# Split-float projections of a decoder step: three products per tile, or high-part products first

## The reference

```
h = rms_norm(x, g_pre_mix);  z = h @ w_in
o = concat(rms_norm(attention_A(z)), rms_norm(attention_B(z)))
x = x + rms_norm(o @ w_out, g_post_mix)
h = rms_norm(x, g_pre_ffn)
u = h @ w_gate;  up = h @ w_up
c = conv_b + sum(conv_w[j] * u_pad[:, j:j + L] for j in range(3))
x = x + rms_norm((gelu(c) * up) @ w_down, g_post_ffn)
```

## Time and profile before

| | |
|---|---|
| median of three runs | 1191.3 us |
| time of the profiled execution | 1191.31 us |
| its span, first to last instruction | 1189.3 us |
| mean granted TensorE clock | 0.993 |
| TensorE matmul (PE) busy | 1165.3 us, 98%, 9947 matmuls |
| TensorE weight load (PEld) busy | 1133.0 us, 95%, 9947 loads |
| VectorE (DVE) busy | 700.7 us, 59% |
| ScalarE (ACT) busy | 552.8 us, 46% |
| GpSimd (POOL) busy | 105.6 us, 9% |
| HBM read | 216.45 MB, 186 GB/s over the span |

### The profile page before, as it was taken

How to read it: one execution, slowest core, us unless ns; L and a number is a source line. 1 busy time by engine, 2 the same in 40 slices (tenths; PEclk the granted TensorE clock), 3 DMA queues, 4 the chain that set the end, 5 groups by cost and what they waited for, 6 DMA issues and landing times.

```text
span 1189.3 us, 25575 instructions
## 1 busy us (share of the span) xinstructions
PE 1165.3 (98%) x9947; PEld 1133.0 (95%) x9947; DVE 700.7 (59%) x1052; ACT 552.8 (46%) x857; POOL 105.6 (9%) x163
## 2 busy tenths in 40 slices
PE   9999999999999799999999999999999999999995
PEld 8999888988999799999999999999999999999995
DVE  6977565575475966565656565655655444454445
ACT  7545455565455654453444444444444333343331
POOL 0100110110002010010011001100110000020001
PEclk9999999999999899999999999999999999999998
DMA  9646687676555355655555555556555655555551
GB/s 332 191 154 228 236 252 232 210 235 219 169 184 181 106 157 177 205 161 192 161 191 173 180 173 181 179 173 190 176 179 173 212 177 179 181 184 180 176 159 73
DMA packets 59473, 222.21 MB, mean 187 GB/s; under 512 B 7064, under 2 KB 7264, under 8 KB 57312
## 3 DMA queue, kind: packets, MB, share of 16 engines
q1 hardware_dynamic: 55008, 196.53, 51.4%
q0 software_dynamic: 4272, 24.94, 6.3%
q10 hardware_dynamic: 144, 0.05, 0.0%
HBM read 216.45 MB, written 5.00 MB: 186 GB/s over the span
## 4 chain that ended last, share of the span: by engine, by line
PE 95%; DVE 2%; DMA 1%; ACT 1%; issue 0%; SPq 0%; POOL 0%; DVEq 0%; ACTq 0%
PE ps L1136 30%; PE ps L1137 29%; PE ps L1138 29%; PE ps L1309 1%; DMA Vk<-in_vb 1%; PE ps L1227 1%; PE ps L1290 1%; PE ps L1218 1%; PE ps L1216 1%; DMA raw<-in_w_in 1%; DVE wl L679 1%; PE ps L1245 0%; PE ps L1163 0%; DVE yT L983 0%; DVE ps L982 0%
## 5 line engine op out<-in xcount | busy, mean ns | idle before, releaser
L1136 PE MATMUL ps<-hh,wh 128*128 128x264 f32 x2080 | 599.3, 288 | 7.6 <-DVE hl L892 5.8
L1138 PE MATMUL ps<-hh,wl 128*128 128x264 f32 x2080 | 592.4, 285 | 0.0
L1137 PE MATMUL ps<-hl,wh 128*128 128x264 f32 x1952 | 557.0, 285 | 0.0
L679 DVE TENSOR_TENSOR wl<-raw,wh 128x1024 fp32r<-128x1024 f32 x363 | 438.6, 1226 | 186.7 <-ACT wh L423 186.2
L423 ACT CAST wh<-raw 128x1024 fp32r<-128x1024 f32 x363 | 374.8, 1046 | 275.7 <-PE ps L1138 271.6
L1136 PEld LDWEIGHTS ps<-hh,wh 128*128 128x128 f32 x2080 | 393.3, 189 | 19.7 <-issue 17.3
L1138 PEld LDWEIGHTS ps<-hh,wl 128*128 128x128 f32 x2080 | 392.2, 189 | 0.0
L1137 PEld LDWEIGHTS ps<-hl,wh 128*128 128x128 f32 x1952 | 368.1, 189 | 0.1
L1137 PE MATMUL ps<-gl,wh 128*128 (+1 forms) x704 | 200.4, 285 | 0.0
L1136 PE MATMUL ps<-gh,wh 128*128 (+1 forms) x704 | 200.1, 284 | 0.0
L1138 PE MATMUL ps<-gh,wl 128*128 (+1 forms) x704 | 199.6, 283 | 0.0
(11 more groups left out here) (230 smaller groups left out, 830.5 us busy)
## 6 DMA issues: line engine op xcount, KB each, us to landing
raw<-in_w_gate SPq DMA_DIRECT2D x88, 512.0 KB, 3.7
raw<-in_w_up SPq DMA_DIRECT2D x88, 512.0 KB, 4.5
raw<-in_w_down SPq DMA_DIRECT2D x88, 512.0 KB, 3.6
raw<-in_w_in SPq DMA_DIRECT2D x67, 512.0 KB, 4.9
raw<-in_w_out SPq DMA_DIRECT2D x32, 512.0 KB, 3.9
Kt<-in_kb POOLq DMA_DIRECT2D x8, 1284.0 KB, 6.3
Vk<-in_vb POOLq DMA_DIRECT2D x8, 1024.0 KB, 7.1
out_y<-yT SPq DMA_DIRECT2D x8, 264.0 KB, 2.1
```

What stands on the lines that cost most here:

```text
L679: V.tensor_tensor(wl[:, slot], raw[:, slot], wh[:, slot].bitcast(F32), ALU.subtract).then_inc(lo_ready, 1)
L1136: nc.tensor.matmul(out, a, x, start=start, stop=False)
L1137: nc.tensor.matmul(out, a, xl, start=False, stop=False)
L1138: return nc.tensor.matmul(out, b, x, start=False, stop=stop)
```

## The change

The three matmuls of a tile are split into `mm_high` (`wh` by high, then `wl` by high) and `mm_low` (`wh` by low). In `gemm` each k tile does both output tiles' `mm_high` and then both `mm_low`. In `down` a chunk does all eight `mm_high` and then all eight `mm_low`; the waits per m stay before `mm_high`, and the signals of the last chunk of the first half move with `mm_low`. `mm3` is left for the last two chunks of `w_down`, which aren't changed.

```diff
+            def mm_high(out, w, x, start):
+
+                slot, c = w
+                nc.tensor.matmul(out, wh[:, slot, c:c + P], x, start=start, stop=False)
+                nc.tensor.matmul(out, wl[:, slot, c:c + P], x, start=False, stop=False)
+
+            def mm_low(out, w, xl, stop):
+
+                slot, c = w
+                return nc.tensor.matmul(out, wh[:, slot, c:c + P], xl, start=False, stop=stop)
+
...
                     for m in range(2):
-                        ins = mm3(ps[:, bank + m, 0:TOK], (slot, 256 * k + P * m), xh[:, kt0 + k], xl[:, kt0 + k],
-                                  first and k == 0, last and k == 3)
+                        mm_high(ps[:, bank + m, 0:TOK], (slot, 256 * k + P * m), xh[:, kt0 + k], first and k == 0)
+                    for m in range(2):
+                        ins = mm_low(ps[:, bank + m, 0:TOK], (slot, 256 * k + P * m), xl[:, kt0 + k], last and k == 3)
...
                     if first and half == 1:
                         pe.wait_ge(down_v, m + 1)
-                    ins = mm3(ps[:, (m + 4) % 8, 0:TOK], (slot, P * m), gh[:, kt], gl[:, kt], first, last)
+                    mm_high(ps[:, (m + 4) % 8, 0:TOK], (slot, P * m), gh[:, kt], first)
+                for m in range(8):
+                    ins = mm_low(ps[:, (m + 4) % 8, 0:TOK], (slot, P * m), gl[:, kt], last)
                     if last and m < 7:
                         ins.then_inc(down_done, 1)
```

## The result

The changed kernel takes 1194.3 us (median of 20 runs, 1192.42 to 1195.86), against 1191.83 us for the kernel before (median of 20, 1190.36 to 1195.69). The ratio is 1.0016, with a 95% interval of 1.0009 to 1.0023; the two medians are 2.5 us apart, which is 0.21%. So it is slower by some 0.2%, at the edge of the 2.4 us that I had called no change, and clear of zero. The profiled execution took 1193.36 us with a span of 1191.6 us, 2.3 us over the span of before.

The account below looks back on a forecast made before the run. The prediction took TensorE's stream of matmuls to bound the kernel. From 1191.3 us, plus 1.4 at the border between w_down's halves and 0 for the pace, it forecast 1192.7 us, range 1185.0 to 1200.0.

Parts of the forecast that it names:

- TensorE is the bound: Whole kernel: TensorE's matmul row is busy 98% of the span, so any wait there lengthens the time in full.
- Gemm chunks: The 68 + 32 + 176 chunks of gemm: same matmuls, waits and end signals in place, so 0 us apart from the pace.
- From gate and up to down: First down chunk: the wait for up_taken comes sooner, but VectorE's read-out is still early by 0.55 us, so 0 us.
- The border: Between w_down's halves: banks finish later and are wanted sooner, so TensorE waits +1.4 us, bounds 0 and 2.0.
- The clock: TensorE's granted clock: the new idle comes in pieces too short to lower it, so 0 us.
- The pace of all chunks: Mean matmul interval in 364 chunks, less the last two: taken as unchanged, 0 us, with ends -7.3 and +7.3 us.
- case 2: All chunks: the new order settles in the slower matmul pattern, up to 1200.0 us; chance 0.33.
- Rival 3: All chunks: fewer switches between high and low settle matmuls in the quicker pattern, down to 1185.4 us; chance 0.27.
- What would show it: Signs: gate and up repeats each two chunks at 122.4 ns within 0.3; PE wait of 1 to 2 us entering the second half.
- the likeliest case: Whole kernel: the pace keeps its mean and the halves' border costs 1.4 us, 1192.7 us, range 1190.5 to 1194; chance 0.40.

Follow-up runs that it names:

- last_old: Changed kernel with only the last chunk of w_down's first half back in the old order: span 1191.7 us, 6.24 us for the two chunks at the halves' border.
- first_old: Changed kernel with only the first chunk of w_down's second half back in the old order: span 1191.2 us, 6.51 us for the two chunks at the halves' border.
- eq_old: Kernel before with gl moved up by 128 bytes, so gh and gl start alike within 256 bytes: down's halves 125.41 and 119.58 us.
- eq_new: Changed kernel with gl moved up by 128 bytes, so gh and gl start alike within 256 bytes: down's halves 125.41 and 119.59 us.

## Why the prediction was right, point by point

- *TensorE is the bound, so a stall there reaches the end.* Right: the parts account for the 2.3 us.
- *Gemm chunks, 0 us.* Right, and more exactly than I could argue: 491.38 us in both orders. I had split this in two, no engine fed later (sure) and the pace (a guess between ends). The pace term is 0 there because `hh` and `hl` start alike within 256 bytes, which I had not looked at: that zero was luck.
- *From gate and up to down, 0 us.* Right: the down projection starts at 916.14 us in both profiles, and its first chunks are on time.
- *The border, +1.4 us.* Right in mechanism and nearly in size: 1.56. The read-outs' end was forecast 1047.68 - 1041.69 = 5.99 us after the chunk's start and came at 1048.05 - 1042.06 = 5.99. What was missing is the restart: a matmul let go by a wait is followed by the next after 0.22 us, not 0.12 (1048.11 to 1048.33), and the wait ends 0.06 us after the read-out. That is also the 0.1 us by which last_old and first_old lie over their expectations. The wait came as 0.41 us ahead of the first bank and 0.08 to 0.16 us ahead of each of the others, not as 0.16 for each; the sum is the same.
- *The clock, 0 us.* Right: the mean granted clock is 0.993 in both.
- *The pace of all chunks, 0 with ends at -7.3 and +7.3.* Right in the sum, and mis-sized in one part: down became slower by 0.37 and 0.41 us, 0.4 to 0.5 ns per matmul. That is just short of the 0.5 ns which I had named as a sign that case 2 holds, and it is case 2 in small. "By what type of neighbour changes rows give no sign" was true of what I compared, the wrong thing. Rival 3's hope that fewer switches between high and low spare time is refuted by the pair eq_old and eq_new: sixteen switches against two, and the same intervals. The ends were far too wide for what this order did (0.8 us); the layout moved gate and up by 4.4 us. On the page "TensorE: Matmul & The Clock Gate" of the Trainium skill, the section that I took N / 2.4 + 2.5 from calls it the gap of an isolated matmul, and gives 81 ns at 128 columns and 131 at 512 for a stream of load and matmul pairs; I had left that out. The 121 to 123 ns at 264 columns lie between those two, but the page has no value for 264.
- *What would show it.* The pattern that repeats each two chunks is there. The forecast PE wait of 1 to 2 us is not in the view of waits, which has 0.2; it is in the starts.

The time lies 1.6 us over the forecast of 1192.7, and 0.3 over the 1190.5 to 1194 that I had given the likeliest case; it is inside the whole range only. Of the 1.6 us 0.5 is the kernel before, which came out at 1191.83 over 20 runs in place of 1191.3 over three, 0.8 is down's pace and 0.2 the border's restart; 0.1 to 0.2 is left over, less than such medians can tell.

## What to carry to other kernels

When matmuls are grouped by operand, look at the end of the group: banks that were finished one by one are finished together, and whoever reads them out starts later while the next user asks sooner. When a pace varies in a pattern that repeats exactly, as here to 1 or 2 ns, look for its cause in the program: match its period to the strides of the operands before trying other orders. Here the stride of the moving operand was worth 4.4 us of 491, and the order nothing wherever the parts started alike.

## What the runs showed of the hardware that I had not expected

The interval between matmuls of 264 columns went from 116 to 132 ns with where the moving operands start and with what came before, reproducibly to 1 or 2 ns, with the same instructions. Means in gate and up were 122.5 ns with rows of 1056 bytes, 121.4 with rows of 1088 bytes at (reckoned) multiples of 64, and 122.1 with the same rows 32 bytes further on. The page "SBUF — State Buffer" of the Trainium skill, section "Who interferes with whom", has TensorE's two read ports wait for nobody; that says nothing of an effect of the moving operand's place, which these traces show, and they don't show that the port is what makes it. Some 11 to 12.5 ns over the 110 ns of 264 columns at 2.4 GHz remain in every layout tried, and no run here says what they are. They belong to the full clock: right after the idle of 5.8 us, at the granted clock of 0.50, the starts in the kernel before stand 0.22 us apart (394.35 to 396.33 us in nine steps), which is 264 columns at 1.2 GHz and nothing more, and in all fourteen traces alike. A matmul let go by the wait for a bank was followed by the next after 0.20 to 0.23 us in place of 0.12.
